# A seventh expert panel loaded ahead of each mixture-of-experts stage, into the residual's tile

## The chip, the cores and the metric

The kernel runs on one core of one Trainium2 chip. The metric is the device time of one execution in microseconds, lower is better. The time before is 2522.19 us, the median of three runs (2517.98 to 2522.46).

## What is computed

Two transformer blocks of two layers each, 256 tokens of width 1024, all in float32. The part that the change touches stands at the end of each layer of the second block: a layer norm, then a mixture of 32 experts (each token goes to two of them), then another layer norm over the residual plus the experts' sum.

```python
def one_block(args):
    xb, e = args
    hb = jax.nn.silu(xb @ w_gate[e]) * (xb @ w_up[e])
    return hb @ w_down[e]
...
x = layer_norm(DEEPNORM_ALPHA * x + (1 + gt_m) * y, ln_g[l, 0], ln_b[l, 0])
h = x * (1 + sc_f) + sh_f
y = hier_moe(h, ...)
x = layer_norm(DEEPNORM_ALPHA * x + (1 + gt_f) * y, ln_g[l, 1], ln_b[l, 1])
```

The weights of one expert are three matrices of 1024 x 512, 6 MB together; the 32 experts of one layer are 192 MB, and there are two such stages (l = 0 and l = 1).

## The kernel before, in words

**Panels.** The weights of a pair of experts are cut into 12 units of 1 MB (128 partitions x 2048 numbers): units 0 to 3 are the gate matrices, 4 to 7 the up matrices, 8 to 11 the down matrices. The first two pairs of a stage together have units 0 to 23 (pair 1 holds 12 to 23). A stage takes 16 pairs, so 192 units.

**Places for panels.** Twelve places are used over and over, first in, first out: six of `ring` and six of `more` (parts of `rows`, `B8`, `lo_mix`, `wks`, all free during the stage). TensorE adds 1 to the semaphore `w_free` when it has used the panel of such a place, and SyncE's queue (`load_next`, L725 to L729) waits for that count before it issues the next load. Besides, the units named in `ONCE` have places of their own that are loaded once, ahead of the stage, and never handed back: before the change units 7, 11, 20, 21, 22 and 19. TensorE finds them in `expert_unit` (L1116). The load that goes ahead last is unit 19, into `xt`, after the router's product has read `xt` (`rt_pe`, L774).

**Order of a stage.** SyncE issues the opening loads (twelve places and the `ONCE` units), then one load for every place that TensorE hands back. TensorE (`pair`, L1131) does for each pair: gate products, `scatter` of the previous pair's result into four banks, up products, `gather` of inputs for pairs further on (it waits for VectorE's `mo_sel` and `mo_acc`), a transpose of the hidden values, down products. VectorE (`pair`, L2499) does for the even pair `pack` (the one-hot matrix of the next four experts, L2396), then `add_blocks` (four additions of scattered banks, L2481), the hidden values (L2516), two evacuations, and the low half of the result (L2532). These engines' loops over `PAIRS // 4 - 1` follow the first two pairs, which are written out.

**The residual.** `X` holds the normed rows. At the start of a stage it is split into `Xhi` (rounded, one half by VectorE and one by ScalarE, each adding 1 to `mo_hi`) and `Xlo`, the rest (L2464). The gathers read only `Xhi` and `Xlo`. `norm_gain` and `norm_bias` (L2109, L2115) bring `X` itself to the full layer norm, by a multiplication and an addition with rows spread over all partitions; they run on VectorE between the first gathers and the first pair. `X` is next read near the end of the stage (`combine`). `row_done` hands the slot of such a row back (`row_free`); GpSimd's queue (L3141) then loads the next rows into these slots: `gt_f` behind `norm_gain`, the next `ln_g` behind `norm_bias`. Each of these loads writes 512 KB. The loads behind them on that queue belong to the stage's end or later.

Of the kernel before, what the change touches and what calls it, by code (L numbers as in the profile page):

```python
# [12 lines left out]
ALU = mybir.AluOpType  # L13
# [5 lines left out]
TB = SEQ // P  # L19
# [5 lines left out]
LAYERS = 2  # L25
R = 6
MORE, MORE_AT = 6, 5
ONCE = (7, 11, 20, 21, 22, 19)
UNIT = 2048
BANK = 512  # L30
NEG = -1.0e30
# [128 lines left out]
def f32(ap):  # L160

    return ap.bitcast(F32)
# [64 lines left out]
def build(nc, A, out):  # L227
    ctx = ExitStack()
    with ctx:
# [11 lines left out]
        def sem(name):  # L241
            return ctx.enter_context(nc.semaphore(name))
# [3 lines left out]
        X = sb("X", [P, TB, D])  # L246
        xt = sb("xt", [P, KC, SEQ])
# [70 lines left out]
        def tiny(i, n):  # L318
# [11 lines left out]
        spare = sb("spare", [P, 2, UNIT])  # L330
# [10 lines left out]

        once = [B[7][:].rearrange("p a b -> p (a b)"), B[1][:].rearrange("p a b -> p (a b)"),
                nc.alloc_sbuf_tensor_at("B4_B5", [P, UNIT], F32, offset=place["B4"] + 4 * D)[:]] + \
               [spare[:, i, :] for i in range(2)] + [xt[:].rearrange("p k t -> p (k t)")]

        def panel(slot):
            return ring[:, slot, :] if slot < R else more[slot - R]
# [44 lines left out]
        Xhi, Xlo = [Br[i][:].rearrange("p (t k q) -> p t k q", t=TB, k=KC) for i in (6, 0)]  # L392

        def by_chunk(t):

            return X[:, t, :].rearrange("p (q k) -> p k q", k=KC)
# [44 lines left out]


        w_landed = [sem(f"w_landed{i}") for i in range(R + MORE)]
        once_landed = [sem(f"once_landed{i}") for i in range(4)]
        w_free = sem("w_free")
        in_landed = sem("in_landed")
        root_ready = sem("root_ready")
# [83 lines left out]
        mo_hi = sem("mo_hi")  # L531
# [89 lines left out]
        class Chain:  # L621
# [5 lines left out]
            def link(self, ins):  # L627
                self.n += 1
                ins.then_inc(self.s, 1)
                self.eng.wait_ge(self.s, self.n)  # L630
# [13 lines left out]
        def _(sp):  # L644
# [39 lines left out]
            def open_spare(l):  # L684

                for x in (3, 4):
                    i, n = divmod(ONCE[x], 12)
                    w = A[("moe_wgate_2", "moe_wup_2", "moe_wdown_2")[n // 4]][l]
                    sp.dma_start(once[x], w.rearrange("(i e) (p u k) n -> i e u p (k n)", e=2, u=2, p=P)
                                 [i, n % 2, n % 4 // 2]).then_inc(once_landed[3], 16)  # L690

            def finish():
                for h in range(TB):
# [24 lines left out]
            def moe(l):  # L718
                g = A["moe_wgate_2"][l].rearrange("(i e) (p u k) n -> i e u p (k n)", e=2, u=2, p=P)
                u = A["moe_wup_2"][l].rearrange("(i e) (p u k) n -> i e u p (k n)", e=2, u=2, p=P)  # L720
                d = A["moe_wdown_2"][l].rearrange("(i e) (p u c) n -> i e u p (c n)", e=2, u=2, p=P)
                def source(i, n):
                    return (g, u, d)[n // 4][i, n % 2, n % 4 // 2]

                def load_next(i, n):  # L725

                    slot, _, pos = cur.take_expert()
                    sp.wait_ge(w_free, pos - MORE)
                    sp.dma_start(panel(slot), source(i, n)).then_inc(w_landed[slot], 16)  # L729

                opening = [n for n in range(24) if n not in ONCE]
                cur.begin_experts()
                place_of = [cur.take_expert() for _ in range(R + MORE)]

                def open_slot(t):

                    slot, _, _ = place_of[t]
                    i, n = divmod(opening[t], 12)
                    sp.dma_start(panel(slot), source(i, n)).then_inc(w_landed[slot], 16)

                def open_ring(t):

                    pos = place_of[t][2]
                    sp.wait_ge(w_free, pos if t < MORE_AT else pos - MORE)
                    open_slot(t)

                def open_once(x):

                    i, n = divmod(ONCE[x], 12)
                    sp.dma_start(once[x], source(i, n)).then_inc(once_landed[min(x, 3)], 16)  # L750

                for t in (0, 1):
                    open_ring(t)
                if l == 0:
                    sp.wait_ge(tr_src, TRANS_AT["y_r"] + 1)
                    for t in range(MORE_AT, MORE_AT + MORE):
                        open_slot(t)
                    open_once(0)
                    open_once(2)
                else:  # L760
                    sp.wait_ge(at_o, H // 4 * 3)
                    for x in (0, 1, 2, 4):
                        open_slot(MORE_AT + x)
                    open_once(2)
                for t in (2, 3, 4, MORE_AT + MORE):
                    open_ring(t)
                if l:
                    sp.wait_ge(pj_pe, PROJ_DONE[PROJ_AT["wo_f"] + 1] + TB)
                    for x in (3, 5):
                        open_slot(MORE_AT + x)  # L770
                    open_once(0)
                sp.wait_ge(tr_src, TRANS_AT[f"moe{l}"] + 1)
                open_once(1)
                sp.wait_ge(rt_pe, 2 * l + 1)  # L774
                open_once(5)
                for n in opening[R + MORE:]:
                    load_next(1, n - 12)
                with cur.loop(sp, PAIRS - 2, R + MORE, R + MORE) as i:
                    for n in range(12):
                        load_next(i + 2, n)  # L780

                w = [x.rearrange("i e u p q -> (i e) p u q") for x in (g, u, d)]
                with overflowed(sp, l):
                    with sp.Fori(0, N_EXP) as i:
                        sp.wait_ge(ov_step[l], i + 1)
                        for j in range(3):
                            for half in range(2):
                                sp.dma_start(ring[:, 2 * j + half, :], w[j][i, :, half]).then_inc(ov_landed[l], 16)
                    sp.wait_ge(ov_step[l], N_EXP + 1)
# [12 lines left out]
        def _(pe):  # L802
# [313 lines left out]
            def expert_unit(opening, n):  # L1116

                if opening and n in ONCE:
                    x = ONCE.index(n)
                    pe.wait_ge(once_landed[min(x, 3)], (16 if x < 3 else 48) * opening)  # L1120
                    return once[x]
                slot, landed, _ = cur.take_expert()
                pe.wait_ge(w_landed[slot], landed)
                return panel(slot)
# [456 lines left out]
            b = PROJ_AT["forget"]  # L1581
            wait_taken(pe, b - 2)
            pe.wait_ge(fx_z1, 1)
            for h in range(TB):
                o = bank[2 * (b % 2) + h]
                for k in range(KC):
                    t = slice(h * P, (h + 1) * P)
# [460 lines left out]
        def _(dve):  # L2048
            ch = Chain(dve, dve_chain)
            link = ch.link  # L2050
# [58 lines left out]
            def norm_gain(n):  # L2109
                g = row(f"ln_g{n}")  # L2110
                for h in range(TB):
                    ins = dve.tensor_tensor(X[:, h, :], X[:, h, :], g, ALU.mult)
                row_done(ins, f"ln_g{n}")
# [345 lines left out]
            def moe(l):  # L2459
                dve.tensor_copy(Xhi[:, 0, :, :], by_chunk(0)).then_inc(mo_hi, 1)  # L2460
                transposes(f"moe{l}", xt)
                dve.wait_ge(mo_hi, 2 * l + 2)
                for t in range(TB):
                    dve.tensor_tensor(Xlo[:, t, :, :], by_chunk(t), f32(Xhi[:, t, :, :]), ALU.subtract)  # L2464
                route(l)

                def pack(e0):
# [4 lines left out]
                def packed(xe, c, o, v):  # L2472
                    dve.wait_ge(mo_x, v)
                    shifted(f"moe{l}", xe, c, o).then_inc(mo_xd, 1)
# [60 lines left out]
                def quad(n, e0, i=None, first=False, last=False):  # L2535
                    pair(n, 0, e0, i, first, last)
                    pair(n + 1, 1, e0, i, False, last)

                n = PAIRS * l
                for c in (1, 3):  # L2540
                    packed(XeT[0], c, bank[4 + c], 2 * n + c + 1)
                norm_gain(2 * l)
                norm_bias(2 * l)
                quad(n, 4, first=True)
                with dve.Fori(0, PAIRS // 4 - 1) as i:
                    quad(n + 2, i * 8 + 8, i)
                    quad(n + 4, i * 8 + 12, i)
# [2 lines left out]
                for t in range(TB):  # L2550
                    for e in range(2):
                        dve.wait_ge(mo_s, 4 * (n + PAIRS - 1) + 2 * t + e + 1)
                        x = X[:, t, e * BANK:(e + 1) * BANK]
                        dve.tensor_tensor(x, bank[4 + 2 * t + e][:, :], x, ALU.add).then_inc(mo_acc, 1)  # L2554
                        dve.wait_ge(mo_acc, 4 * (n + PAIRS - 1) + 2 * t + e + 1)
                        ins = dve.bn_stats(st[:, t, e, :], x)  # L2556
                link(ins)
                with overflowed(dve, l):
# [6 lines left out]
                    with dve.Fori(0, N_EXP) as i:  # L2565
# [3 lines left out]
                        for t in range(TB):  # L2569
                            dve.wait_ge(ov_y[l], i * 2 + (t + 1))  # L2570
                            for j in range(2):
                                y = Yacc[:, t, j * BANK:(j + 1) * BANK]
                                ins = dve.scalar_tensor_tensor(out=y, in0=bank[6 + j][:, :],
                                                               scalar=rt_gate[:, t, bass.ds(i, 1)], in1=y,
                                                               op0=ALU.mult, op1=ALU.add)
# [5 lines left out]
                    for t in range(TB):  # L2581
# [6 lines left out]
                        for e in range(2):  # L2588
                            ins = dve.bn_stats(st[:, t, e, :], X[:, t, e * BANK:(e + 1) * BANK])
# [79 lines left out]
            for h in range(TB):  # L2669
                ins = dve.scalar_tensor_tensor(out=Xn[:, h, :], in0=X[:, h, :], scalar=rms_i[0][:, h:h + 1],  # L2670
                                               in1=sc, op0=ALU.mult, op1=ALU.mult)
# [282 lines left out]
            b = PROJ_AT["forget"]  # L2954
# [263 lines left out]
```

## Time and profile before

| what | value |
|---|---|
| median of three runs | 2522.19 us |
| the profiled execution's own time | 2519.59 us |
| its span on the core | 2517.9 us |
| TensorE busy | 2374.3 us (94%) |
| VectorE busy | 1269.4 us (50%) |
| ScalarE busy | 740.3 us (29%) |
| GpSimd busy | 156.4 us (6%) |
| DMA moved | 690.76 MB, mean 274 GB/s |
| the two expert stages, about | 1380 to 1835 us and 2041 to 2500 us of the span |

The profiled execution is 2.6 us under the median. TensorE's share says little in the expert stages, since a matmul that waits in the pipeline counts as busy; there the DMA's share and GB/s, slice by slice, and the chain of waits are to be read. The first stage looks like the second at all places named here.

### The profile page before, as it was taken

To read this page: it belongs to the slowest core of one execution; us is meant where nothing else is said; L and a number is where in the kernel's file an instruction comes from. 1 tells how busy PE (TensorE), PEld (TensorE's weight loads), DVE (VectorE), ACT (ScalarE), POOL (GpSimd) and SP (SyncE) were. 2 spreads that over 40 slices of the span, in tenths; PEclk is the share of its full clock that TensorE was granted. 3 is DMA by queue.
4 is the path that set the end of the run, shared out by engine and by line. 5 is a ranking of instruction groups with operands and counts; after the bars stand their busy time and mean duration, and the time that the engine had idled before them with its cause. 6 is when DMAs were issued, how large, how long until landed. Compare 5 with 4: busy or idle time off the path is not lost. (4 is left out here: it accounts for less than half of the span.)

```text
span 2517.9 us, 40112 instructions
## 1 busy us (share of the span) xinstructions
PE 2374.3 (94%) x16068; PEld 1628.9 (65%) x16068; DVE 1269.4 (50%) x1883; ACT 740.3 (29%) x1089; POOL 156.4 (6%) x250
## 2 busy tenths in 40 slices
PE   8999999999999999999999999899889999999985
PEld 8997789978997799844884444333357754443432
DVE  7864578746876685545465222122177552221213
ACT  4334543344335543312221111111036421111111
POOL 1100001000110010020240000000000000000000
PEclk9999999999999999999999999999989999999999
DMA  8766347755874285443106899999965379999996
GB/s 344 303 249 209 127 173 302 273 204 190 326 279 149 87 315 197 153 145 127 37 4 245 343 423 423 424 424 423 421 248 184 130 313 390 422 424 424 424 424 272
DMA packets 109219, 690.76 MB, mean 274 GB/s; under 512 B 14780, under 2 KB 16124, under 8 KB 34216
## 3 DMA queue, kind: packets, MB, share of 16 engines
q1 hardware_dynamic: 88720, 618.10, 62.1%
q0 software_dynamic: 20320, 70.85, 7.7%
q8 instruction: 91, 1.49, 0.2%
q14 instruction: 32, 0.26, 0.0%
q10 hardware_dynamic: 56, 0.06, 0.0%
HBM read 687.85 MB, written 1.11 MB: 274 GB/s over the span
## 5 line engine op out<-in xcount | busy, mean ns | idle before, releaser
L818 PE MATMUL bank<-ring,B 128*64 128x512 f32 (+1 forms) x1712 | 536.6, 599 | 24.3 <-DMA ring<-in_moe_wup 13.9
L2180 DVE TENSOR_TENSOR ring_r<-ring,B_r 128x2048 fp32r<-128x2048 f32 x181 | 410.6, 2288 | 220.9 <-ACT B_r L1709 220.4
L818 PE MATMUL bank<-B_r 128*128 128x512 f32 (+1 forms) x1916 | 497.0, 347 | 7.8 <-DVE B_r L2532 6.0
L1709 ACT ACTIVATE B_r<-ring 128x2048 fp32r<-128x2048 f32 x184 | 347.0, 1909 | 274.7 <-PE bank L818 272.8
L818 PE MATMUL bank<-xt_r,B_r 128*128 128x256 f32 x1408 | 396.4, 282 | 3.9 <-DVE ring_r L2180 2.4
L818 PE MATMUL bank<-xt_r,ring_r 128*128 128x256 f32 x1408 | 395.8, 282 | 0.0
L818 PEld LDWEIGHTS bank<-B_r 128*128 128x128 f32 x1916 | 324.9, 189 | 101.0 <-issue 47.1
L818 PEld LDWEIGHTS bank<-ring,B 128*64 128x64 f32 (+1 forms) x1712 | 177.8, 143 | 275.1 <-issue 258.7
L818 PEld LDWEIGHTS bank<-xt_r,B_r 128*128 128x128 f32 x1408 | 267.3, 190 | 7.7 <-issue 6.2
L818 PEld LDWEIGHTS bank<-xt_r,ring_r 128*128 128x128 f32 x1408 | 267.4, 190 | 0.0
L818 PE MATMUL bank<-B 64*64 64x64 f32 (+6 forms) x2544 | 236.5, 286 | 26.1 <-DMA rows<-in_moe_wgate 15.0
L818 PE MATMUL bank<-wks,B 128*64 128x512 f32 (+1 forms) x608 | 224.1, 518 | 0.8 <-DVE B L2877 0.8
L818 PE MATMUL bank<-rows,B 128*64 128x512 f32 x496 | 222.4, 594 | 0.3
L818 PEld LDWEIGHTS bank<-B 64*64 64x64 f32 (+4 forms) x2544 | 139.4, 148 | 112.6 <-issue 94.2
L818 PE MATMUL bank<-lo_mix_r,B_r 128*128 128x256 f32 x704 | 195.5, 281 | 0.4 <-DVE lo_mix_r L2200 0.4
L2481 DVE TENSOR_TENSOR B<-bank,B 128x512 f32<-128x512 f32 x112 | 69.6, 684 | 193.2 <-PE bank L818 193.2
L2532 DVE TENSOR_TENSOR B_r<-bank,B_r 128x512 fp32r<-128x512 f32 x60 | 38.7, 686 | 241.7 <-ACT B_r L1828 241.7
L818 PE MATMUL bank<-B_r,xt_r 128*128 128x512 f32 (+1 forms) x368 | 143.5, 392 | 3.7 <-DVE xt_r L2148 1.3
L2516 DVE SCALAR_TENSOR_TENSOR B<-B,bank 128x512 f32<-128x512 f32 x32 | 36.5, 1140 | 211.0 <-issue 173.8
L818 PE MATMUL bank<-ring_r,xt_r 128*128 128x512 f32 x352 | 139.6, 397 | 0.0
L818 PE MATMUL bank<-ring_r,B_r 128*128 128x512 f32 x352 | 138.3, 393 | 0.0
L818 PEld LDWEIGHTS bank<-lo_mix_r,B_r 128*128 128x128 f32 x704 | 132.0, 189 | 2.1 <-DVE lo_mix_r L2200 0.6
(373 smaller groups left out, 2830.1 us busy)
## 6 DMA issues: line engine op xcount, KB each, us to landing
ring<-in_moe_wup SPq DMA_DIRECT2D x92, 1024.0 KB, 23.4
ring<-in_moe_wdown SPq DMA_DIRECT2D x84, 1024.0 KB, 21.5
ring<-in_ffn_w_gate SPq DMA_DIRECT2D x44, 1024.0 KB, 4.9
ring<-in_ffn_w_up SPq DMA_DIRECT2D x44, 1024.0 KB, 7.4
ring<-in_ffn_w_down SPq DMA_DIRECT2D x44, 1024.0 KB, 7.5
wks<-in_ada_w POOLq DMA_DIRECT2D x72, 512.0 KB, 6.1
rows<-in_moe_wdown SPq DMA_DIRECT2D x32, 1024.0 KB, 23.5
wks<-in_moe_wgate SPq DMA_DIRECT2D x30, 1024.0 KB, 25.2
```

What stands on the lines that cost most here:

```text
L818: ins = pe.matmul(out, lhsT, rhs, start=start, stop=stop, skip_group_check=True)
L1709: act.activation(hi, ring[:, slot, :], ACT.Copy).then_inc(sp_hi, 1)
L2180: dve.tensor_tensor(ring_r[:, slot, :], ring[:, slot, :], f32(hi), ALU.subtract).then_inc(sp_lo, 1)
L2481: ins = dve.tensor_copy(y, b) if begin else dve.tensor_tensor(y, b, y, ALU.add)
L2516: dve.scalar_tensor_tensor(out=strided(m_h, 4), in0=natural(m_sg, 4), scalar=m_slot[(n // 2) % 2][:, j:j + 1], in1=natural(bank[1][:, :], ...
L2532: dve.tensor_tensor(ye_lo[:, c], scaled_y(d) if scale else bank[2 + d][:, :], f32(ye_hi[:, c]), ALU.subtract).then_inc(mo_yl, 1)
```

## The change

`ONCE` gets a seventh unit, number 18, whose place is `X` itself. SyncE issues its load behind that of `xt`, once `Xlo` is written (a third count of `mo_hi`). Behind the first two pairs VectorE rebuilds `X` as `Xhi` + `Xlo`, and `norm_gain` and `norm_bias` move from ahead of these pairs to behind the rebuild. The number of units that go through the twelve places falls from 186 to 185 per stage. The semaphores of the `ONCE` units are grouped anew: units 7 and 11 share one, 20 has one, the other four share the third.

```diff
-ONCE = (7, 11, 20, 21, 22, 19)
+ONCE = (7, 11, 20, 21, 22, 19, 18)
...
-               [spare[:, i, :] for i in range(2)] + [xt[:].rearrange("p k t -> p (k t)")]
+               [spare[:, i, :] for i in range(2)] + [xt[:].rearrange("p k t -> p (k t)"), X[:].rearrange("p a b -> p (a b)")]
+
+        def landed_at(x):
+
+            return max(x - 1, 0) if x < 3 else 2
...
                 sp.wait_ge(rt_pe, 2 * l + 1)
                 open_once(5)
+                sp.wait_ge(mo_hi, 3 * l + 3)
+                open_once(6)
...
-                    pe.wait_ge(once_landed[min(x, 3)], (16 if x < 3 else 48) * opening)
+                    pe.wait_ge(once_landed[landed_at(x)], (32, 32, 16, 64)[min(x, 3)] * opening)
...
-                dve.wait_ge(mo_hi, 2 * l + 2)
+                dve.wait_ge(mo_hi, 3 * l + 2)
                 for t in range(TB):
-                    dve.tensor_tensor(Xlo[:, t, :, :], by_chunk(t), f32(Xhi[:, t, :, :]), ALU.subtract)
+                    ins = dve.tensor_tensor(Xlo[:, t, :, :], by_chunk(t), f32(Xhi[:, t, :, :]), ALU.subtract)
+                ins.then_inc(mo_hi, 1)
                 route(l)
...
+                quad(n, 4, first=True)
+                for t in range(TB):
+                    ins = dve.tensor_tensor(by_chunk(t), f32(Xhi[:, t, :, :]), f32(Xlo[:, t, :, :]), ALU.add)
+                link(ins)
                 norm_gain(2 * l)
                 norm_bias(2 * l)
-                quad(n, 4, first=True)
```

VectorE, in a stage, from the last of the first gathers' evacuations on. Before (`X<-X,rows` are `norm_gain` and `norm_bias`, the row that waits for `mo_gt` is `pack`, L2532 ends a pair):

```order
1073 L2148 TENSOR_SCALAR B<-bank,cols 128x256
1074 L2112 TENSOR_TENSOR X<-X,rows 128x1024 [waits row_landed5]
1075 L2112 TENSOR_TENSOR X<-X,rows 128x1024
1076 L2118 TENSOR_TENSOR X<-X,rows 128x1024 [waits row_landed4,row_free5]
1077 L2118 TENSOR_TENSOR X<-X,rows 128x1024
1078 L2396 TENSOR_TENSOR B_r<-const,B 128x512 [waits mo_gt,mo_x,row_free4]
```

With the change, from the low halves of the second pair to the `pack` of the loop's first pair:

```order
1086 L2539 TENSOR_TENSOR B_r<-bank,B_r 128x512 [waits mo_ye]
1087 L2551 TENSOR_TENSOR X<-B_r 128x8x128 x2
1088 L2118 TENSOR_TENSOR X<-X,rows 128x1024 [waits row_landed5,dve_chain]
1089 L2118 TENSOR_TENSOR X<-X,rows 128x1024
1090 L2124 TENSOR_TENSOR X<-X,rows 128x1024 [waits row_landed4,row_free5]
1091 L2124 TENSOR_TENSOR X<-X,rows 128x1024
1092 L2555 UNCONDITIONAL_BRANCH [waits row_free4]
1093 L2555 ISA
1094 L2513 ISA [waits mo_x]
1095 L2402 ISA [waits mo_gt]
1096 L2402 TENSOR_TENSOR B_r<-const,B 128x512
```

Four instructions moved from ahead of the first `pack` to ahead of the second one, and two new ones stand ahead of them. The hand-back of the two row slots moves with them, and so do the two loads of GpSimd's queue that wait for it (its own order is unchanged).

SyncE's queue at the end of the opening, before:

```order
118 L750 DMA B<-in_moe_wdown 128x2048 [waits tr_src]
119 L750 DMA xt<-in_moe_wup 128x2048 [waits rt_pe]
120 L729 DMA ring<-in_moe_wgate 128x2048 [waits w_free] x2
121 L729 DMA ring<-in_moe_wup 128x2048 [waits w_free] x3
122 L729 DMA rows<-in_moe_wdown 128x2048 [waits w_free]
```

With the change:

```order
118 L754 DMA B<-in_moe_wdown 128x2048 [waits tr_src]
119 L754 DMA xt<-in_moe_wup 128x2048 [waits rt_pe]
120 L754 DMA X<-in_moe_wup 128x2048 [waits mo_hi]
121 L733 DMA ring<-in_moe_wgate 128x2048 [waits w_free] x2
122 L733 DMA ring<-in_moe_wup 128x2048 [waits w_free] x2
123 L733 DMA ring<-in_moe_wdown 128x2048 [waits w_free]
```

One load of an up panel now goes into `X` ahead of the stage; it is missing from those that wait for a place.

## Rows read from the trace of the kernel before

**Rows 1.** Chain that ended last, second stage: start us, us, what.

```profile
2118.97 25.11 PE bank L818 x120
2145.39 25.11 PE bank L818 x120
...
2250.48 25.32 DMA ring<-in_moe_wup
...
2280.18 25.33 DMA ring<-in_moe_wup
```

**Rows 2.** Windows, second stage: stretch, us, busy by engine, PEclk, DMA share, GB/s.

```profile
2040.00:2050.00 10.00, 8.80 (x58) 6.18 (x58) 6.09 (x15) 2.04 (x4) 0.00 (x0) 1.00 0.10 42
...
2095.00:2097.50 2.50, 2.50 (x14) 0.86 (x12) 0.00 (x0) 0.00 (x0) 0.00 (x0) 1.00 0.96 400
2097.50:2100.00 2.50, 2.50 (x16) 0.80 (x12) 0.00 (x0) 0.30 (x1) 0.00 (x0) 1.00 0.08 33
2100.00:2102.50 2.50, 2.50 (x16) 0.79 (x14) 1.97 (x4) 0.79 (x2) 0.00 (x0) 1.00 0.39 75
2102.50:2105.00 2.50, 2.50 (x14) 0.85 (x12) 0.00 (x0) 0.00 (x0) 0.00 (x0) 1.00 1.01 387
...
2120.00:2130.00 10.00, 10.00 (x50) 3.45 (x48) 1.29 (x2) 1.08 (x2) 0.00 (x0) 1.00 1.02 428
...
2200.00:2210.00 10.00, 10.00 (x50) 4.11 (x48) 1.98 (x4) 1.09 (x2) 0.00 (x0) 1.00 1.01 424
```

**Rows 3.** Timeline of SyncE's queue, second stage: start us, us, line, DMA, how many.

```profile
2034.43 0.33 SPq L750 DMA_DIRECT2D xt<-in_moe_wup  x1
2051.34 0.80 SPq L729 DMA_DIRECT2D ring<-in_moe_wgate  x2
...
2085.93 3.77 SPq L729 DMA_DIRECT2D ring<-in_moe_wdown  x3
2100.54 0.33 SPq L729 DMA_DIRECT2D rows<-in_moe_wdown  x1
...
2112.67 3.88 SPq L729 DMA_DIRECT2D ring<-in_moe_wup  x3
2122.64 3.77 SPq L729 DMA_DIRECT2D ring<-in_moe_wdown  x3
```

**Rows 4.** Windows, first stage, the place that answers to the gap of Rows 2.

```profile
1435.00:1437.50 2.50, 2.50 (x14) 0.86 (x12) 0.00 (x0) 0.00 (x0) 0.00 (x0) 1.00 0.78 324
1437.50:1440.00 2.50, 2.50 (x14) 0.86 (x12) 0.54 (x1) 1.09 (x2) 0.00 (x0) 1.00 0.07 23
1440.00:1442.50 2.50, 2.50 (x15) 0.81 (x12) 1.44 (x4) 0.00 (x0) 0.00 (x0) 1.00 0.69 203
```

**Rows 5.** Timeline of VectorE, second stage: Xlo, gain, bias, end of pair, pack, additions.

```profile
2029.57 3.94 DVE L2464 TENSOR_TENSOR B_r<-X,B_r 128x1024 fp32r<-128x1024 f32 x2
...
2047.51 2.35 DVE L2112 TENSOR_TENSOR X<-X,rows 128x1024 f32<-128x1024 f32 x2
2049.89 2.36 DVE L2118 TENSOR_TENSOR X<-X,rows 128x1024 f32<-128x1024 f32 x2
...
2100.40 1.29 DVE L2532 TENSOR_TENSOR B_r<-bank,B_r 128x512 fp32r<-128x512 f32 x2 [7.92 <-ACT B_r L1828]
2101.61 0.68 DVE L2396 TENSOR_TENSOR B_r<-const,B 128x512 fp32r<-128x512 f32 x1
...
2107.22 2.48 DVE L2481 TENSOR_TENSOR B<-bank,B 128x512 f32<-128x512 f32 x4 [4.85 <-PE bank L818]
```

**Rows 6.** Timeline of GpSimd's queue, second stage: the two row loads.

```profile
2050.40 0.54 POOL L3141 DMA_DIRECT2D rows<-mod_rows  x1 [25.59 <-DVE X L2112]
2052.55 0.53 POOL L3141 DMA_DIRECT2D rows<-in_ln_g  x1 [1.61 <-DVE X L2118]
```

**Rows 7.** DMA queues over the whole span: packets, MB, share of 16 engines.

```profile
q0 software_dynamic: 20320, 70.85, 7.7%
```

**Rows 8.** Timeline of TensorE, second stage: the third pair's gather.

```profile
2115.51 2.17 PE L818 MATMUL bank<-B_r 128*128 128x256 f32 x16
```

More of the change, by code:

```diff
@@ L443, in build @@
         w_landed = [sem(f"w_landed{i}") for i in range(R + MORE)]
-        once_landed = [sem(f"once_landed{i}") for i in range(4)]
+        once_landed = [sem(f"once_landed{i}") for i in range(3)]
         w_free = sem("w_free")
@@ L689, in open_spare @@
                     sp.dma_start(once[x], w.rearrange("(i e) (p u k) n -> i e u p (k n)", e=2, u=2, p=P)
-                                 [i, n % 2, n % 4 // 2]).then_inc(once_landed[3], 16)
+                                 [i, n % 2, n % 4 // 2]).then_inc(once_landed[2], 16)
             def finish():
@@ L749, in open_once @@
                     i, n = divmod(ONCE[x], 12)
-                    sp.dma_start(once[x], source(i, n)).then_inc(once_landed[min(x, 3)], 16)
+                    sp.dma_start(once[x], source(i, n)).then_inc(once_landed[landed_at(x)], 16)
                 for t in (0, 1):
```

## The prediction

> **What bounds the kernel now.** I read the chain that ended last first. In the second expert stage it runs over TensorE for some six pairs, 2118.97 to 2145.39 for one, so 26.42 us a pair; then it runs over panels landing, from 2250.48 to 2280.18, so 29.70 us a pair [rows 1]. A pair is 12 panels: a panel costs the DMA 29.70 / 12 = 2.475 us, and TensorE 2.20 us. TensorE is the faster of the two, begins with a lead of loaded panels, eats it up, and then waits for DMA to the end. So the windows come second: from 2102.5 on the DMA share is 1.01 with some 424 GB/s, in the stretch where TensorE still runs freely as well as later [rows 2]. The stage therefore ends when the stream that starts at about 2101.5 has brought its last panel. What counts is the start of that stream and how much it has to bring, and anything else that is put into it.
>
> Third, what is ahead of that start. The windows show a gap: shares 0.96, 0.08 and 0.39 between 2095 and 2102.5, so (0.04 + 0.92 + 0.61) x 2.5 = 3.9 us without work [rows 2]. SyncE's queue says why: after the three loads that begin at 2085.93 it issues nothing until 2100.54 [rows 3]. Units 19 to 22 are in `ONCE`, so TensorE hands no place back while it uses them; the load at 2100.54 waits for unit 23. In this stretch TensorE is the limit (busy 2.50 of 2.50 in each window [rows 2]), and the DMA had run dry. The first stage has the same gap: (0.22 + 0.93 + 0.31) x 2.5 = 3.7 us [rows 4].
>
> **The seventh panel.** Its load is issued behind that of `xt` at 2034.43 [rows 3]; `Xlo` is written at 2029.57 + 3.94 = 2033.5 [rows 5], so the new wait on SyncE is over before it begins and holds back nothing. The DMA is nearly idle then (share 0.10 in 2040 to 2050 [rows 2]), so it lands by about 2044, 40 us ahead of its use. Cost: zero, covered by that idle stretch.
>
> What does it save? Before, 192 - 6 - 12 = 174 panels go through handed-back places, 17 of them issued from 2051.34 to the group of 2085.93 [rows 3], so 157 remain for the stream that starts with unit 23. With the change there are 173, but unit 18 is no longer handed back either, so only 16 are issued ahead of the gap: 157 remain again. The stream starts when TensorE has used unit 23, at the same moment as before. The saved 2.475 us only make the gap longer. Gain: zero in either stage. Putting it otherwise, when unit 23 has been used, twelve places can be full and no more, however many panels came ahead.
>
> Here stands a rule of the Trainium skill that speaks for the change: "DMA: Bandwidth & Descriptors", section "Rules for kernel authors", wants a DMA issued early and waited for late. By that rule the stage would end one panel earlier; the gap that the rows show says that the early load is not on the path. I keep it as a rival.
>
> **What moves along.** VectorE hands back the two row slots behind `norm_gain` and `norm_bias`. Before, the two row loads of 512 KB were issued at 2050.40 and 2052.55 [rows 6], ahead of the gap, where 2 x 512 KB more or less only changed how long the DMA sat dry. As a check: 17 x 2.475 + 2 x 1.24 = 44.6 us from about 2052.3 end at 2097, where the gap begins. With the change they are issued when the moved instructions are done, at about 2108 and 2110.5 (worked out below). That is inside the stream that sets the end, where the share is already 1.01 and nothing is free. So the stage gets longer by their transfer.
>
> Price of one: half a panel's bytes, so half of 2.475, 1.24 us. The upper bound is the software queue's own share: 7.7% of 2517.9 us for 70.85 MB is 2.74 us per MB [rows 7], 1.43 us for 0.524 MB. The lower bound is zero, if this queue's packets fit between the others. I take 1.24, since the share of 1.01 at 424 GB/s leaves bytes as the measure [rows 2]. Two rows and two stages: 4 x 1.24 = 4.95 us (5.7 at the upper bound).
>
> The Trainium skill, "DMA: Bandwidth & Descriptors", section "Specifications", puts the HBM limit of a core at about 358 GB/s; a row would then cost 1.46 us and the sum be 5.9. The stream's 424 GB/s [rows 2] decide against that.
>
> Is there idle time further on that would take this in? Between 2100.54 and the end of the group of 2112.67 nine loads are issued; 9 x 2.475 = 22.3 us from 2101.5 end at 2123.8. The next is issued at 2122.64 [rows 3] and, with the lag of 1 us that the first shows, starts at 2123.6. The stream just about never breaks; the window there reads 1.02 [rows 2]. So there is nothing to absorb 2.5 us, apart from perhaps 0.2.
>
> **VectorE behind the first two pairs.** The four moved instructions take 2.35 + 2.36 us; the stretch they leave, at 2047.51, is followed by idle time, and nobody gains. The two rebuilding additions are not in the trace: from below the contiguous ones, 1.18 each; from above twice the strided subtraction that makes `Xlo`, so 3.94 each. I take the subtraction's own 1.97, an instruction of the same size and one strided side [rows 5]. They start at 2100.40 + 1.29 = 2101.69: rebuild to 2105.6, gain to 2108.0, bias to 2110.4, `pack` to 2111.2 (0.68 and a small copy), four additions 2.48 to 2113.7. Queued behind them are the hidden values, which VectorE starts now once TensorE's up products end, when the gather begins at 2115.51 [rows 8]. TensorE waits there for `pack` (4.3 us early) and for the first additions (3 us early). Slack of the whole row: 1.8 us, so cost zero; the idle 4.85 us ahead of the additions [rows 5] is the cover. At 3.94 each, the row ends 2.1 us late, and TensorE hands places back that much later; but by then the stream carries 2.5 us of row loads as a backlog, so even that breaks nothing.
>
> The rest is free: units 7 and 11 now share a semaphore, but both loads are issued ahead of `xt`'s; the last count for the fourth group waits for the panel in `X`, landed 40 us before; `gt_f` is needed 380 us later.
>
> **Sum.** Panel 0, rows 2 x 2.475 = +4.95, VectorE 0: from the profiled execution's 2519.59 it is 2524.5; that execution lies 2.6 under the median, and from the median of 2522.19 it is 2527.1. A measurement of this kernel can tell 0.2%, 5.04 us, from no change: the forecast falls almost on that line.
>
> **Rivals.** (1) *The early panel counts*: the stage ends 2.475 us earlier, and the rows ride along free: 2522.19 - 4.95 = 2517.2. For it: the bytes of the final stream would have to be fewer. Against: the count of 157 on both sides and the two gaps. 6%. (2) *The early panel counts and the rows cost what I say*: both are 4.95 us, 2522.2. 9%. (3) *Neither counts*: the rows' packets fit in, 2522.2. Against it: the share of 1.01. 7%. By the Trainium skill, "DMA: Bandwidth & Descriptors", section "Issuing engines are not separate DMA queues", loads of all queues share the same 16 engines; by that rule this rival falls. (4) *VectorE becomes the bound behind the first two pairs*, the slower side: with rebuilding additions beyond 2.9 us each the hidden values of the third pair come late, and beyond 4.1 the delay is longer than the rows' backlog and opens a second gap at 2123.8. At 5 us each the row is 4.2 us late, 1.7 more than the backlog: 2.475 + 1.7 a stage, +8.4, 2530.6. For it: a strided write that nothing in the trace prices. Against: the strided read at 1.97. 8%.
>
> **How the numbers follow.** The forecast has 70%. It splits on the line of 5.04 us: a price of 1.24 and a little absorbed is under it, a price nearer 1.43 over it; 34% under, 36% over. Faster: rival 1, 6%. Within 0.2%: 34 + 9 + 7 = 50%. Slower: 36 + 8 = 44%. The range goes from 2521.0, which takes in rivals 2 and 3 at 2522.2, to 2530.8, which takes in the upper price (2527.9) and rival 4; the forecast alone would have 2524.5 to 2528.
>
> **What would show it.** In the changed profile: a load into `X` right behind `xt`; a gap of about 3.9 + 2.5 + 2.5 = 8.9 us ahead of unit 23 instead of 3.9, with the stream starting at the same distance from the stage's first product; the two row loads issued some 6 and 9 us behind the second pair's end; TensorE's gather of the third pair unmoved; the stage's end about 2.5 us later, twice. It would be wrong if TensorE reached unit 23 sooner, if the gap stayed at 4 us, or if the third pair took longer than 26.4 us.

## The result, and the profile after

| what | before | after |
|---|---|---|
| median of 20 runs | 2520.24 us (2516.18 to 2524.23) | 2524.24 us (2517.44 to 2527.95) |
| ratio, with its 95% interval | | 1.0015 (1.0008 to 1.0022) |
| span of the profiled execution | 2517.9 us | 2520.0 us |

The change made the kernel slower by about 3.8 us (0.0015 x 2520), 2.0 to 5.5 by the interval. The forecast was 2527.1, that is 4.95 us over the median of three then known; 2524.24 lies in the range. It also lies under the line of 0.2%, on which the forecast nearly fell; the interval holds the forecast's 4.95 as well, so the times alone do not tell 3.8 from it. The two spans differ by only 2.1 us, but the stretch between the two expert stages alone (the first stage's last scatter to the second's first product) took 205.2 us in the trace of before and 202.9 in that of after, and between 202.9 and 205.7 in the eleven kernels below. So I read each stage against its own first product: 1386.75 and 2047.69 us before, 1386.89 and 2047.14 after. In the second stage these are, before and after:

```profile
2047.69 7.09 PE L818 MATMUL bank<-ring,B 128*64 128x512 f32 x32 [1.14 <-issue]
```

```profile
2047.14 7.09 PE L824 MATMUL bank<-ring,B 128*64 128x512 f32 x32 [1.14 <-issue]
```

**The gap grew, the stream did not start sooner.** The windows of after, second stage (stretch, us, busy by engine, clock, DMA share, GB/s), to be held against [rows 2]:

```profile
2040.00:2050.00 10.00, 8.81 (x59) 6.07 (x59) 3.71 (x12) 2.04 (x4) 0.00 (x0) 1.00 0.47 197
...
2092.50:2095.00 2.50, 2.50 (x14) 0.86 (x12) 0.00 (x0) 0.00 (x0) 0.00 (x0) 1.00 0.67 282
2095.00:2097.50 2.50, 2.50 (x14) 0.86 (x12) 0.00 (x0) 0.00 (x0) 0.00 (x0) 1.00 0.02 7
2097.50:2100.00 2.50, 2.50 (x14) 0.86 (x12) 0.13 (x1) 0.83 (x2) 0.00 (x0) 1.00 0.00 0
2100.00:2102.50 2.50, 2.50 (x14) 0.83 (x12) 2.50 (x3) 0.26 (x1) 0.00 (x0) 1.00 0.62 128
2102.50:2105.00 2.50, 2.50 (x16) 0.79 (x14) 2.47 (x2) 0.00 (x0) 0.00 (x0) 1.00 1.03 383
...
2110.00:2112.50 2.50, 2.50 (x14) 0.86 (x12) 2.30 (x5) 0.00 (x0) 0.53 (x1) 1.00 1.00 421
```

The seventh panel moves in the nearly idle stretch: 197 GB/s in 2040 to 2050 where it was 42. The gap is now (0.33 + 0.98 + 1.00 + 0.38) x 2.5 = 6.7 us, before 3.9. TensorE is busy 2.50 of 2.50 in each of these windows, as before. The load that waits for unit 23 is issued 2100.01 - 2047.14 = 52.87 us after the stage's first product; before it was 2100.54 - 2047.69 = 52.85 [rows 3]. SyncE's queue in after:

```profile
2035.25 0.33 SPq L754 DMA_DIRECT2D xt<-in_moe_wup  x1
2035.62 1.52 SPq L754 DMA_DIRECT2D X<-in_moe_wup  x1
...
2100.01 0.33 SPq L733 DMA_DIRECT2D ring<-in_moe_wdown  x1
```

**The whole opening in one row.** A window over 56 us (from 4 to 60 us behind the first product) and one over the 340 us behind it give the bytes. Second stage, before:

```profile
2051.69:2107.69 56.00, 55.74 (x301) 23.72 (x298) 11.84 (x20) 10.22 (x22) 0.53 (x1) 1.00 0.93 376
2107.69:2447.69 340.00, 316.78 (x1604) 139.83 (x1602) 73.94 (x118) 44.09 (x95) 0.00 (x0) 1.00 1.01 423
```

and after:

```profile
2051.14:2107.14 56.00, 55.74 (x301) 23.70 (x298) 16.07 (x20) 10.22 (x22) 0.00 (x0) 1.00 0.85 339
2107.14:2447.14 340.00, 314.73 (x1592) 133.02 (x1593) 77.66 (x123) 44.12 (x95) 1.07 (x2) 1.00 1.01 423
```

(376 - 339) x 56 us = 2.07 MB less in the opening: the panel (1.05 MB) and the two rows (2 x 0.52). Then both run at 1.01 and 423 GB/s; there is no room in which the rows could be made up for. POOL's two issues (1.07 us, x2) are in the second window now. The panel need not be moved any more; the other 1.02 MB have to be moved later, 2.4 us at 423 GB/s.

**The row loads and VectorE.** GpSimd's queue and VectorE's, after, against [rows 6] and [rows 5]:

```profile
2107.91 0.54 POOL L3151 DMA_DIRECT2D rows<-mod_rows  x1 [81.93 <-DVE X L2118]
2110.06 0.53 POOL L3151 DMA_DIRECT2D rows<-in_ln_g  x1 [1.61 <-DVE X L2124]
```

```profile
2099.87 1.29 DVE L2539 TENSOR_TENSOR B_r<-bank,B_r 128x512 fp32r<-128x512 f32 x2 [7.92 <-ACT B_r L1834]
2101.08 3.90 DVE L2551 TENSOR_TENSOR X<-B_r 128x1024 f32<-128x1024 f32 x2
2105.01 2.36 DVE L2118 TENSOR_TENSOR X<-X,rows 128x1024 f32<-128x1024 f32 x2
2107.40 2.36 DVE L2124 TENSOR_TENSOR X<-X,rows 128x1024 f32<-128x1024 f32 x2
2110.20 0.69 DVE L2402 TENSOR_TENSOR B_r<-const,B 128x512 fp32r<-128x512 f32 x1 [0.44 <-DVE X L2124]
...
2110.88 2.48 DVE L2488 TENSOR_TENSOR B<-bank,B 128x512 f32<-128x512 f32 x4
2115.12 1.14 DVE L2523 SCALAR_TENSOR_TENSOR B<-B,bank 128x512 f32<-128x512 f32 x1 [1.76 <-PE bank L824]
```

The rebuild takes 1.95 us for each addition, the row of work ends at 2113.4, and the hidden values still wait 1.76 us for TensorE. That is the slack of 1.8 us.

**Where the stage ends.** TensorE's last up products start when the last up panel has landed. In before and in after, second stage:

```profile
2485.17 3.65 PE L818 MATMUL bank<-ring,B 128*64 128x512 f32 x16 [1.89 <-DMA ring<-in_moe_wup]
```

```profile
2486.60 3.65 PE L824 MATMUL bank<-ring,B 128*64 128x512 f32 x16 [1.19 <-DMA ring<-in_moe_wup]
```

From the stage's first product that is 437.48 us before and 439.46 after: 1.98 us later; in the first stage 1.62 (437.63 and 439.25). The sum, 3.6, agrees with the 3.8 us that the runs show. I use this point, and not the very last scatter, because what lies behind it jumps by 1.5 us for another reason (the last section).

### The profile page after: what moved, and what is told of

Read it like the earlier page. It is cut to its first block, busy times and chain, and to the rows that moved or that the text cites. A ratio compares the mean times of both kernels' runs of the same rounds, so it can differ in the third digit from the quotient of the medians.

```text
span 2520.0 us, 40133 instructions
## 1 busy us (share of the span) xinstructions
PE 2371.7 (94%) x16068; PEld 1622.8 (64%) x16068; DVE 1277.2 (51%) x1887; ACT 740.6 (29%) x1089; POOL 156.8 (6%) x250
## 4 chain that ended last, share of the span: by engine, by line
PE 69%; DMA 20%; DVE 6%; issue 2%; ACT 2%; SPq 0%; DVEq 0%; ACTq 0%
PE bank L824 67%; DMA ring<-in_moe_wup 10%; DMA B<-in_moe_wgate 9%; PE bank L822 2%; DMA ring<-in_moe_wdown 1%; ACT B L1775 1%; DVE ring_r L2186 0%; DVE xt_r L2167 0%; ACT B L1825 0%; DVE B L2703 0%; DVE lo_mix_r L2206 0%; DVE B L2336 0%; ACT B_r L1715 0%; DVE B L2887 0%; DVE X L2564 0%
## 5 line engine op out<-in xcount | busy, mean ns | idle before, releaser
L824 PE MATMUL bank<-ring,B 128*64 128x512 f32 (+1 forms) x1712 | 439.5, 601 | 21.9 <-DMA ring<-in_moe_wup 12.0
L824 PEld LDWEIGHTS bank<-ring,B 128*64 128x64 f32 (+1 forms) x1712 | 152.8, 144 | 271.9 <-issue 254.1
L824 PE MATMUL bank<-rows,B 128*64 128x512 f32 x480 | 215.5, 594 | 41.7 <-DMA lo_mix<-in_moe_wgate 25.5
L824 PEld LDWEIGHTS bank<-rows,B 128*64 128x64 f32 x480 | 62.2, 137 | 176.1 <-issue 175.7
```

The source lines that it names most:

```text
L824: ins = pe.matmul(out, lhsT, rhs, start=start, stop=stop, skip_group_check=True)
```

## The experiments

The table gives each kernel against runs of before in the same comparison, and beside it, from its one trace, by how much later than in before the last up products start, first and second stage.

| kernel | median, before's median | ratio (95%) | last up products, us |
|---|---|---|---|
| after | 2524.24, 2520.24 | 1.0015 (1.0008 to 1.0022) | +1.62, +1.98 |
| e1_move_norm_only | 2524.74, 2519.95 | 1.0019 (1.0010 to 1.0028) | +2.74, +2.83 |
| e2_five_once | 2517.88, 2519.95 | 0.9990 (0.9981 to 0.9999) | -0.58, -0.28 |
| e3_four_once | 2518.87, 2519.95 | 0.9994 (0.9985 to 1.0004) | -0.53, +0.09 |
| e4_short_rows | 2520.04, 2519.95 | 1.0000 (0.9990 to 1.0011) | +0.77, +0.95 |
| e5_sixteen_places | 2508.24, 2520.80 | 0.9950 (0.9934 to 0.9967) | -5.99, -5.77 |
| e6_sixteen_and_X | 2511.48, 2520.80 | 0.9966 (0.9955 to 0.9978) | -4.18, -5.15 |
| e7_rows_twice_in_stream | 2531.04, 2521.82 | 1.0034 (1.0023 to 1.0045) | +4.13, +5.18 |
| e8_rows_twice_ahead | 2521.29, 2521.82 | 0.9995 (0.9985 to 1.0005) | +0.14, -0.11 |
| e9_after_third_row_late | 2522.18, 2521.11 | 1.0005 (0.9996 to 1.0014) | +1.23, +1.47 |
| e10_before_third_row_late | 2517.13, 2521.11 | 0.9985 (0.9975 to 0.9994) | -1.94, -1.05 |
| e11_sixteen_third_row_late | 2509.03, 2521.11 | 0.9952 (0.9939 to 0.9966) | -5.96, -5.74 |

The two stages' sums follow the differences of the medians within 1.7 us everywhere. The theory is the prediction's own: the early panel brings nothing, and a row load costs what it takes only inside the saturated stream.

**One part alone: only the norm is moved.** Six panels, nothing rebuilt:

```diff
+                quad(n, 4, first=True)
                 norm_gain(2 * l)
                 norm_bias(2 * l)
-                quad(n, 4, first=True)
```

> The kernel before, with six panels ahead as it was, and only norm_gain and norm_bias moved behind the first two pairs (X is intact, so nothing is rebuilt). Stream theory (a stage ends when the stream that starts with unit 23 is through, and the two row loads that the move pushes into this stream are its only cost): two rows at half a panel each and a little more, 2.5 to 2.6 us a stage, so +4 to +5.2 us against before; gap ahead of unit 23 some 6.4 us instead of 3.9. Early-panel theory (a panel loaded ahead saves its 2.475 us a stage, and the changed kernel's +0.15% is that gain less larger losses): without the panel the move alone costs 3.8 + 4.95, about +8.8 us. Theory that the rebuilding additions on VectorE cost the time: 0, as they are not there.

Measured: +4.8 us. The moved rows alone cost at least as much as the whole change; the seventh panel and the rebuild add nothing to the loss.

**Fewer early panels.** The same count from the other side: five, then four units of their own instead of six (before otherwise).

```diff
-ONCE = (7, 11, 20, 21, 22, 19)
+ONCE = (7, 11, 20, 21, 22)
```

> The kernel before, with five panels ahead instead of six: unit 19 goes through the twelve places like the rest. Stream theory: the gap of 3.9 us shrinks by 2.475 to about 1.4 us, the stream still starts with unit 23 and has 157 panels, time within 1 us of before. Early-panel theory: one panel fewer ahead, +2.475 us a stage, +4.95 us.

```diff
-ONCE = (7, 11, 20, 21, 22, 19)
+ONCE = (7, 11, 20, 21)
```

> The kernel before, with four panels ahead: units 19 and 22 go through the twelve places. Stream theory: two panels are more than the gap of 3.9 us holds, so the gap closes and 2 x 2.475 - 3.9 = 1.05 us a stage are lost, +2.1 us in all. Early-panel theory: +9.9 us.

Measured, by the medians: -2.1 and -1.1 us; no loss with one panel less, none with two. The opening of e2, second stage:

```profile
2049.44:2105.44 56.00, 55.73 (x301) 23.72 (x298) 11.84 (x20) 10.22 (x22) 0.53 (x1) 1.00 0.97 396
```

396 GB/s where it was 376: 20 x 56 = 1.1 MB more, the panel that is not loaded ahead is simply loaded in the gap. With four (e3) the gap is closed:

```profile
2049.03:2105.03 56.00, 55.74 (x301) 23.72 (x298) 11.83 (x20) 10.22 (x22) 0.53 (x1) 1.00 1.00 403
```

That is 27 x 56 = 1.5 MB more than before, against two panels, 2.1 MB, so 0.6 MB or 1.4 us are left for later. I had expected +2.1 us in all, which did not come: a miss. The third row load of the stage (the next `ln_b`, L3139 there) had moved, which I had not looked at. In e3, second stage:

```profile
2500.19 0.53 POOL L3139 DMA_DIRECT2D rows<-in_ln_b  x1 [449.78 <-PE bank L816]
```

That is 455.16 us after the first product, behind the whole stream; in before it is issued at 425.62. Half a panel less in the stream is 1.24 us, about what was left over. The 2 us of e2 I can explain only in part: its last up products give 0.9 of them. In the first stage four small loads stand behind the third row on GpSimd's queue (`forget_w` and three more, 136 KB in all). In before they are issued from 425.74 us after the first product on, in e2 from 454.70 on, behind the whole stream; that stage gains 0.58 us, the second, which has no such loads, 0.28.

**The rows' transfer taken away.** The changed kernel, its two row loads cut to the first 8 of 1024 numbers:

```diff
-                pool.dma_start(bc[ROW_SLOT[n]], row_source(name).partition_broadcast(P)).then_inc(row_landed[ROW_SLOT[n]], 16)
+                w = 8 if name in ("gt_f0", "ln_g1", "gt_f1", "ln_g3") else D
+                pool.dma_start(bc[ROW_SLOT[n]][:, 0:w], row_source(name)[0:w].partition_broadcast(P)).then_inc(row_landed[ROW_SLOT[n]], 16)
```

> The changed kernel, in which the two row loads of each stage (gt_f and the ln_g behind it) bring only the first 8 of their 1024 numbers, so that their transfer is left out; everything else, the rebuilding and the order on all engines, stays. Stream theory: the 2.6 us a stage go away, so about 5 us less than the changed kernel, and -1.5 to 0 us against before. Theory that VectorE's rebuilding costs the time, and early-panel theory: the row loads are hidden, +3.8 us against before as the changed kernel has it.

Measured: no difference to before by the times, with an interval of -2.5 to +2.8 us; so at least a large part of the loss is in these loads. The trace leaves more of it: the last up products are 0.77 and 0.95 us late where in after they are 1.62 and 1.98. By it a short load still costs about half of a long one, where the stream theory had the whole loss gone; the times cannot decide between the two. The windows at the place where the short loads run, second stage, bear the trace out:

```profile
2110.74:2112.74 2.00, 2.00 (x12) 0.71 (x10) 1.56 (x4) 0.00 (x0) 0.54 (x1) 1.00 1.00 422
2112.74:2114.74 2.00, 2.00 (x12) 0.58 (x10) 2.00 (x4) 0.00 (x0) 0.00 (x0) 1.00 1.20 272
2114.74:2116.74 2.00, 2.00 (x11) 0.61 (x8) 0.24 (x2) 0.00 (x0) 0.00 (x0) 1.00 0.82 300
2116.74:2118.74 2.00, 2.00 (x18) 2.00 (x19) 1.12 (x1) 0.92 (x2) 0.00 (x0) 1.00 1.02 427
```

Over these four microseconds the DMA engines are busy (1.20 and 0.82), but (424 - 272) x 2 + (424 - 300) x 2 = 0.55 MB less comes in than at the stream's 424 GB/s: 1.3 us of the stream, about half of the 2.475 that two full rows should take.

**The rows doubled, inside the stream and ahead of it.** Each of the two loads is made twice, once in the changed kernel, once in the kernel before:

```diff
+                if name in ("gt_f0", "ln_g1", "gt_f1", "ln_g3"):
+                    first[0] += 16
+                    pool.dma_start(bc[ROW_SLOT[n]], row_source(name).partition_broadcast(P)).then_inc(done, 16)
+                    pool.wait_ge(done, first[0])
```

> The changed kernel, with each of the two row loads of a stage made twice, the second behind the landing of the first. Stream theory: four rows instead of two in the stream, 2.5 us more a stage, so +8.5 to +9 us against before, twice the cost of the changed kernel or a little more. If the cost of the changed kernel lies in VectorE's order and not in these loads: +3.8 us, as it is.

> The kernel before, with each of the two row loads of a stage made twice, at the place where it makes them, ahead of the gap. Stream theory: the additional 2.5 us of transfer shrink the gap from 3.9 to about 1.4 us and cost nothing, within 1 us of before. If row loads cost their transfer wherever they stand: +5 us.

Measured: +8.6 us by the ratio in the one place, -1.3 with an interval that reaches +1.3 in the other. The same 2 MB more cost 8.6 - 3.8 = 4.8 us, more than the change's own loss, behind the gap and nothing ahead of it. Their openings, second stage, e7 and then e8:

```profile
2057.52:2113.52 56.00, 55.74 (x301) 23.72 (x298) 16.09 (x20) 10.22 (x22) 0.00 (x0) 1.00 0.86 340
```

```profile
2054.63:2110.63 56.00, 55.73 (x301) 23.72 (x298) 11.84 (x20) 10.22 (x22) 1.58 (x3) 1.00 0.97 395
```

In e8 the doubled rows are in the opening, 395 GB/s for 376, and only the gap shrinks. The Trainium skill, "DMA: Bandwidth & Descriptors", section "Issuing engines are not separate DMA queues", lets the loads of all queues share the same engines; e7 agrees, with 8.6 us for loads of a queue that carries no panels.

**What would shorten the stage: places that come back.** The same 18 panels ahead, but sixteen rotating places instead of twelve: the places of units 19 to 22 are handed back as well.

```diff
-MORE, MORE_AT = 6, 5
-ONCE = (7, 11, 20, 21, 22, 19)
+MORE, MORE_AT = 10, 5
+ONCE = (7, 11)
...
-                with cur.loop(sp, PAIRS - 2, R + MORE, R + MORE) as i:
+                with cur.loop(sp, PAIRS // 4 - 1, 48, R + MORE) as i:
```

> The kernel before, with the same 18 panels loaded ahead of a stage, but with sixteen places that are handed back and two that are not (units 7 and 11), instead of twelve and six: the two halves of spare, the middle of B4 and B5, and xt are used over and over. Stream theory: places are handed back through the whole opening, so the DMA never runs dry and the stream starts with unit 0 (about 1 us behind the first hand-back at 2051.3) instead of unit 23; it has 174 panels and two rows, 2052.3 + 174 x 2.475 + 2.5 = 2485.5 instead of about 2490.5, so 4.6 to 5 us a stage, -9 to -10 us in all, and no gap at unit 23. Early-panel theory (only the number of panels ahead counts, and it is the same 18): 0 us.

and the same with the change on top (unit 18 in `X`, the rebuild, the moved norm):

> The sixteen places, and on top of them the change under study: unit 18 ahead into X, X rebuilt behind the first two pairs, gain and bias moved there. Stream theory: now the stream runs from unit 0 on without a break, so the early panel is worth its 2.475 us a stage, and the row loads, which lie in the stream at either place, cost nothing more: 2.5 us a stage less than with sixteen places alone, so -14 to -15 us against before. If the panel is worth nothing anywhere: the same -9 to -10 us as with sixteen places alone, or 4 to 5 us slower than these if the moved rows cost what they cost in the changed kernel.

Measured: -12.6 us by the ratio for e5, which beats both kernels, and more than the 9 to 10 expected of the places. Not all of it is theirs: e5 also renumbers the wait of the stage's third row load (the next `ln_b`), which slides from 425.62 to 431.59 us after the first product and, as the next experiment shows, counts no more there. Between e11 and e10 below, which both hold that row back until the stream is through, the difference is 8.1 us by the medians (2517.13 - 2509.03) and 8.7 by the last up products: that is what the places are worth. e6 is 3.2 us slower than e5 by the medians, where I had expected 5 faster or, at worst, 4 to 5 slower; the intervals of the two overlap, but the last up products are later in both stages. The case that I held likelier fell. The openings, second stage, e5 and then e6:

```profile
2046.47:2102.47 56.00, 55.73 (x301) 23.71 (x298) 11.82 (x20) 10.23 (x22) 0.53 (x1) 1.00 1.01 413
```

```profile
2048.77:2104.77 56.00, 55.74 (x301) 23.70 (x298) 16.03 (x20) 10.23 (x22) 0.00 (x0) 1.00 0.96 391
```

In e5 no gap is left (1.01). I took that to mean that a further early panel would count. But unit 18 is then no longer handed back, so a load less is issued in the opening and it runs dry again: (1.01 - 0.96) x 56 = 2.8 us, more than a panel's 2.475. In bytes, (413 - 391) x 56 = 1.23 MB less are moved there, against the 1.05 MB of the panel that need not be; that makes 0.18 MB, 0.4 us a stage. The last up products are 1.81 and 0.62 us later than in e5, so a part of the loss stays without a name.

**The third row.** What e3 had shown by accident, made on purpose: the next `ln_b` waits until the stage's last panel has been used, in the changed kernel, in before and in e5. In the first stage the four small loads behind it on the queue (136 KB) slide with it.

```diff
-                    pool.wait_ge(w_free, MOE_AT[int(name[4]) // 2] + last_use(2) + R)
+                    pool.wait_ge(w_free, MOE_AT[int(name[4]) // 2] + EXPERT_UNITS + R)
```

> The changed kernel; the third row load of each stage (512 KB, the next ln_b) waits until the stage's last panel has been used, so it stands behind the stream instead of among its last panels (issued about 455 us after the stage's first product instead of 433). Theory (each row load among the stream's panels costs its 1.24 us, and in the changed kernel this one has slid so far back that only a part of it still counts): against the kernel before +2.5 us (4.95 for the two rows in both stages, less 2.48 for the third row). Rival, the third row has no part in the time and the two rows simply cost 3.8: +3.8. Third: the row now comes too late for the closing layer norm: +5 or more.

> The kernel before with the same late third row load and nothing else. Theory: each of the two stages gets shorter by the row's 1.24 us, -2.5 us, and the difference to the changed kernel with the late row is the full 4.95. Rival, the third row has no part in the time: 0. Third: it comes too late: +1 or more.

> The kernel with sixteen rotating places (2508.2 us, ratio 0.9950) with the late third row load. Theory: -2.5 us more, ratio about 0.994. Rival: 0.995 as it was, if the third row has no part in the time.

Measured: +1.3 us (-1.0 to +3.5 by the interval), -3.8 (-6.3 to -1.5) and no gain over e5. So the third row is paid for in before. The two kernels with the row held back differ by 2522.18 - 2517.13 = 5.05 us, next to the forecast's 4.95. That they meet so closely is in part luck: each median comes from 11 runs spread over 9 us, which by an estimate from that scatter leaves the difference uncertain by some 3 us. Their last up products, second stage, e10 and then e9:

```profile
2478.83 3.65 PE L818 MATMUL bank<-ring,B 128*64 128x512 f32 x16 [0.90 <-DMA ring<-in_moe_wup]
```

```profile
2489.69 3.65 PE L824 MATMUL bank<-ring,B 128*64 128x512 f32 x16 [0.71 <-DMA ring<-in_moe_wup]
```

436.43 and 438.95 us after the first products (2042.40 and 2050.74): 2.52 us apart, for a panel's worth of rows. In the first stage it is 3.17. For e11 I had expected 2.5 us more: a miss. In e5 that load was issued 431.59 us after the first product, and the last up products started at 431.71, so it stood behind the last up panel already.

## Why the prediction was right

- **The early panel, zero.** Right. The load behind unit 23 is issued 52.87 us after the first product instead of 52.85, and one early panel less (e2) costs nothing. That it was without any effect is not right: see the sum, below.
- **Rival 1, the early panel counts, and rival 2.** Both fall: they give -5 and 0 us, and the runs 2.0 to 5.5. And e1, without the seventh panel, is 1 us slower than the change, where a panel that counts would make it 4.95 slower. The Trainium skill, "DMA: Bandwidth & Descriptors", section "Rules for kernel authors", wants a load issued early; here that saved nothing, since the place does not come back and the panel only left a longer gap.
- **Rival 3, the rows fit in.** Falls with e7 against e8: the same bytes cost 8.6 us behind the gap and nothing ahead.
- **Rival 4, VectorE.** Falls: the strided write takes 1.95 us, not 5; the slack of 1.8 us is 1.76 in the trace. TensorE's gather of the third pair is at 2114.97, 67.83 us after the first product, before 67.82 [rows 8]. The pair takes 26.23 us in the chain, before 26.42 [rows 1]:

```profile
2114.97 2.17 PE L824 MATMUL bank<-B_r 128*128 128x256 f32 x16
```

```profile
2118.27 25.11 PE bank L824 x120
2144.50 25.11 PE bank L824 x120
...
2238.00 25.19 DMA B<-in_moe_wgate
...
2267.73 25.15 DMA B<-in_moe_wgate
```

- **The gap of 8.9 us.** Right in bytes, wrong in place. By the opening's rows, (1.01 - 0.85) x 56 = 9.0 us are dry, before 4.5. But only 6.7 lie ahead of unit 23, because some two microseconds of what is missing fall into holes further up.
- **The sum, 4.95 us.** The mechanism was right, and the term for the two rows agrees in size: 5.05 us between e9 and e10, within their noise. The step that does not hold is "The rest is free". The third row load, which stands among the stage's last panels and not behind them, waits for the 176th place handed back. With one more unit that hands nothing back, this is the 183rd panel used instead of the 182nd, and the load slides from 425.62 to 433.17 us after the first product (in the first stage from 425.22 to 432.87). Before and after:

```profile
2473.31 0.53 POOL L3141 DMA_DIRECT2D rows<-in_ln_b  x1 [420.23 <-PE bank L818]
```

```profile
2480.31 0.53 POOL L3151 DMA_DIRECT2D rows<-in_ln_b  x1 [369.72 <-PE bank L824]
```

In before that row (in the first stage together with the four small loads behind it) delayed the last up products by 1.94 and 1.05 us (e10 against before), in after by 0.39 and 0.51 (e9 against after). So the change gives back 1.55 + 0.54 = 2.1 us by these traces, 1.1 by the medians (5.05 less the 4.00 between the kernels with it). e1 bears on this: it moves the two rows as well, but keeps six panels, so its third row stays where before has it, some 12 us ahead of the last up products where after has 6:

```profile
2476.65 0.53 POOL L3141 DMA_DIRECT2D rows<-in_ln_b  x1 [368.73 <-PE bank L818]
```

That is 428.22 us after its first product (2048.43), in the first stage 427.92. Its last up products are 2.74 and 2.83 us late, and its time is +4.8 us: the rows' price with nothing given back. By the traces, then, the third row makes the difference between the forecast and the measured 3.8. By the times it is not shown: their interval holds 4.95 too, and 1.1 us is less than the scatter of the medians that it is taken from. The result would have stayed within 0.2% with the forecast's 4.95 as well, since the line is at 5.04.

## What to carry to other kernels

In a stage that a stream of loads ends, count what is left for the stream when its places first come back to it; a load in a place that never comes back lengthens the dry stretch ahead and leaves that number as it was, while more places that do come back took about 8 us off here (e11 against e10). When code moves, follow each load that its hand-backs release and every wait on a count that the change renumbers, also those on other queues: a transfer is free in a dry stretch and costs its full length in a saturated one. Push what the stream does not need behind its last panels.

## What the runs showed of the hardware

**TensorE's clock at a stage's end.** The stage's closing part jumps between two lengths: the last down products (x32) take 7.3 us or 8.78, or the last up products (x16) 3.65 or 5.35. In after, first stage, they take 8.78 from 1832.44 on; windows of one microsecond:

```profile
1830.00:1831.00 1.00, 0.00 (x0) 0.00 (x0) 0.98 (x1) 0.00 (x0) 0.00 (x0) 1.00 1.01 420
1831.00:1832.00 1.00, 0.63 (x4) 0.42 (x4) 0.10 (x1) 0.21 (x1) 0.00 (x0) 1.00 1.02 426
1832.00:1833.00 1.00, 0.56 (x4) 0.24 (x6) 0.97 (x2) 0.39 (x1) 0.00 (x0) 0.94 1.06 442
1833.00:1834.00 1.00, 1.00 (x6) 0.39 (x4) 0.97 (x2) 0.00 (x0) 0.00 (x0) 0.50 0.96 401
...
1835.00:1836.00 1.00, 1.00 (x4) 0.24 (x2) 0.97 (x2) 0.00 (x0) 0.00 (x0) 0.50 1.09 442
1836.00:1837.00 1.00, 1.00 (x6) 0.29 (x4) 0.93 (x3) 0.00 (x0) 0.00 (x0) 0.86 0.98 410
1837.00:1838.00 1.00, 1.00 (x6) 0.31 (x4) 0.68 (x1) 0.00 (x0) 0.00 (x0) 1.00 1.01 410
```

The engine had stood idle through 1830 to 1831 and been half busy for two microseconds more; then the granted clock is 0.50, the level of 1.2 GHz, for some three microseconds, and full again. It costs 1.5 us. In before and in after it came in the first stage and not in the second, in e10 and e9 in the second and not in the first. That is scatter of two fifths of the effect under study, and the last scatter alone would have told the wrong story about e10's second stage (0.45 us later than before, though its panels were 1.05 us earlier).

**Short loads in a full stream.** Two row loads of 8 numbers for each of 128 partitions kept about half the delay of two loads of 1024 numbers (0.77 and 0.95 us a stage, of 1.62 and 1.98). What they cost is not their bytes: in the four microseconds in which they run, the DMA engines are busy (1.20 and 0.82 in the windows of e4) while the rate falls from 422 GB/s to 272 and 300. They take the engines' time; no run here shows on what it goes, and the times of e4 (0.0, -2.5 to +2.8 us) do not resolve it.

**A strided write.** The rebuild's addition over 128x1024 numbers with a strided result takes 1.95 us, as long as the subtraction with a strided input (1.97); `norm_gain`, with no stride, takes 1.18 [rows 5].

**The bandwidth.** The stream holds 423 GB/s for 340 us. The Trainium skill, "DMA: Bandwidth & Descriptors", section "Specifications", puts a core's limit at HBM at about 358, as half of a stack's 716 for two cores; for this program on one core the rows show more, and no run here has two cores at once.
